# Attention of a hybrid decoder layer: the values become the weights of the probability-times-value product, two heads in the two halves of the array's columns

## The chip, the cores and the metric

The kernel runs on one core of a Trainium2 chip. The metric is the device time of one launch in microseconds (us), the median of several runs. A profiled execution of the same program gives the trace that is read here.

## What is computed

One layer of a decoder, on 1024 prompt tokens and 8 sample tokens, all in float32:

```
z = RMSNorm(x) @ w_in            # q | k | v (12 heads x 64) | u | v_sg | gate_a | gate_b
A: 3 head groups of 4 heads, (window, dilation) = (128,1), (512,4), (2048,16)
   each query reads 129 strided keys; p = softmax(q k / 8); o = p v
   the groups are merged per head slot: y = sum_g softmax_g(logsumexp_g) * o_g
B: gelu(u) * (W_s LayerNorm(gelu(v_sg)) + b)
m = sigmoid(gate_a) * (A @ w_proj_attn) + sigmoid(gate_b) * (B @ w_proj_sg)
x = x + RMSNorm(m @ w_out);  x = x + RMSNorm(SwiGLU(RMSNorm(x)))
```

The change touches only `o = p v` of the prompt tokens and the merge of the groups.

## The kernel before, in words

Every large product runs as three matmuls (high times high, low times high, high times low part, lines 477 to 479 and 894 to 904), which keeps float32 accuracy. These fill TensorE nearly the whole time; what is special to attention is threaded between them.

Attention runs twice, once for each pair of head slots (`pair` 0 and 1); e = 0, 1 is the head of the pair, and lies on partitions 0 to 63 or 64 to 127 of the transposed tensors. The dilated groups 1 and 2 share one order of tokens (residue r of 4, two halves of 128), so that a step T = 0..7 holds 128 queries of group 0 ("near") and 128 queries of groups 1 and 2 together ("far"). For each step T:

- `scores(T)` on TensorE: keys times queries, the two heads in the two halves of the array's rows (lines 620, 624);
- `maxima(T, e)` on VectorE adds the mask, takes the row maxima, and writes the scores into `pr`; `probs(T, e)` on ScalarE is the exponential, in place, with the row sums into `st_at`;
- `turns(T, e)` on TensorE transposes the 3, 4 or 6 blocks of probabilities into PSUM (`psT`); `copy0` and `copy1` on ScalarE bring them to `prT`;
- `pv(T, e)` on TensorE, line 664: weights are the probability block, 128 x 128, and the values, 64 columns, are the moving operand. There are 3 matmuls of a head for T = 0, 4 for T = 2, 4, 6, and 6 for odd T. The trace shows each float32 matmul as two records;
- `outputs(T, e)` on VectorE copies near and far outputs to `ob`, queries on partitions.

Between these, `gates` (24 chunks of three matmuls for each quarter of the gate projection, in groups of three chunks) keeps TensorE busy: nine matmuls stand between `turns(T, 1)` and `pv(T, 0)`. `gate` on ScalarE takes the tanh of a finished gate tile, `gated` on VectorE multiplies it in and, at each third tile, makes the low part of the next weights (`lo_in`, line 1500).

After each pair the near outputs have to be brought into the order of tokens of the far ones. `merge_near` transposes the near `ob` (8 tiles) and the statistics (8 small ones); `merge_place` transposes both back with a stride, which puts them in the far order; VectorE computes the weights of the groups (`merge_weights`, then `merge_sum` after an exponential on ScalarE), multiplies and adds; `merge_out` transposes the sum (8 tiles), and ScalarE writes it to `oaT` in token order. These steps are put between the jobs (j, tg) of the next projection: merge_near after job (0, 1), merge_place after (1, 0), merge_out after (2, 1).

In the second pair VectorE has the sample tokens' key products as well (`k_scores`, lines 1733 and 1735, 24 of them), whose caches GpSimd loads by DMA (line 2086) as products are done, each request behind a wait on `s_kq`; the value caches (line 2098) follow in the same queue. TensorE needs all 24 products after job (3, 2) and all value caches in job (4, 2) (line 805).

What sets the order is the code of each engine, written out by hand; the waits are semaphores.

Of the kernel before, what the change touches and what calls it, by code (L numbers as in the profile page):

```python
# [19 lines left out]
P = 128  # L20
# [96 lines left out]
def build(nc, A, O):  # L117
# [19 lines left out]
    with ctx:  # L137
# [45 lines left out]
        assert _o <= R[4]  # L183
        o0T, _ = at("o0T", [P, SEQ], F32, pr_at)
        srow, _ = at("srow", [4, SEQ], F32, prT_at)
        cv, _o = at("cv", [P, 24, 256], F32, R[3] + 2 * NT * 4)
        assert _o <= R[4]
# [280 lines left out]
        def _(pe):  # L468
# [137 lines left out]
            def attention(pair, U, M):  # L606
# [41 lines left out]

                def pv(T, e):
                    r, hh, N = T // 2, T % 2, 16 * pair + 2 * T + e  # L650
                    hd = slice(HD * e, HD * e + HD)
                    pe.wait_ge(at_c0, N + 1)
                    pe.wait_ge(at_c1, N + 1)
                    if T:
                        pe.wait_ge(at_o, N - 1)
                    if T < 7:

                        pe.wait_ge(at_m, N + 3)
                    near = [vtok[:, t, hd] for t in ((T - 1, T) if T else (T,))]
                    far = [vtok[:, 8 * g + 4 * q + r, hd] for g in (1, 2) for q in range(hh + 1)]  # L660
# [6 lines left out]
                    ins.then_inc(at_pv, 1)  # L667

# [20 lines left out]
                for T in range(8):  # L689
                    gates(12 * T)  # L690
                    if T < 7:
                        scores(T + 1)
                    gates(12 * T + 3)
                    turns(T, 0)
                    gates(12 * T + 6)
                    turns(T, 1)
                    gates(12 * T + 9)
                    pv(T, 0)
                    pv(T, 1)

# [3 lines left out]
            def merge_near(pair):  # L704

                pe.wait_ge(at_o, 16 * pair + 16)
                if pair:
                    pe.wait_ge(s_nc, 5)
                for t in range(8):
                    ins = turn(psT[t // 4][:, P * (t % 4):P * (t % 4) + P], ob[:, 0, t, :])  # L710
                    if t % 4 == 3:
                        ins.then_inc(mg_t, 1)
                for t in range(8):
                    ins = turn(psR[t // 4][0:4, P * (t % 4):P * (t % 4) + P], st_at[:, 0, t, :])
                    if t % 4 == 3:
                        ins.then_inc(mg_t, 1)

            def merge_place(pair):

                pe.wait_ge(mg_a, 2 * pair + 2)  # L720
                pe.wait_ge(mg_d, 2 * pair + 2)
# [4 lines left out]
                for t in range(8):  # L726
                    first = 512 * (t % 2) + t // 2
                    ins = turn(psT[t // 4][:, P * (t % 4):P * (t % 4) + P], o0T[:, first:512 * (t % 2) + 512:4])
                ins.then_inc(mg_p, 1)
# [267 lines left out]
        def _(act):  # L997
# [140 lines left out]
            def attention(pair, U, M):  # L1138
# [33 lines left out]
                for T in range(8):  # L1172
# [3 lines left out]
                    copy1(T, 0)  # L1176
                    if T < 7:
                        probs(T + 1, 0)
# [4 lines left out]
                    if T < 7:  # L1183
                        probs(T + 1, 1)
                    if T % 2:
                        gate((12 * T + 11) // KD)

            def merge_copy(pair):
                act.wait_ge(mg_t, 4 * pair + 1)
                fn(o0T[:, 0:512], psT[0][:, :], ACT.Copy).then_inc(mg_a, 1)  # L1190
                act.wait_ge(mg_t, 4 * pair + 3)
                fn(srow[:, 0:512], psA[0:4, :], ACT.Copy).then_inc(mg_a, 1)
# [4 lines left out]

            def merge_back(pair):
                for hh in range(2):
                    act.wait_ge(mg_o, 2 * pair + hh + 1)  # L1200
                    fn(oaT[:, pair, 512 * hh:512 * hh + 512].rearrange("p (i r) -> p r i", r=4), by4(psR[hh][:, :]), ACT.Copy
                       ).then_inc(mg_done, 1)

            def merge_in(pair, j, tg):
                if (j, tg) == (0, 1):
                    merge_copy(pair)
                elif (j, tg) == (1, 1):
                    merge_exp(pair)
                elif (j, tg) == (2, 1):
                    merge_back(pair)  # L1210

# [278 lines left out]
        def _(dve):  # L1490
# [109 lines left out]
            def attention(pair, U, M):  # L1600
# [27 lines left out]
                def outputs(T, e):  # L1628
                    N = 16 * pair + 2 * T + e
                    dve.wait_ge(at_pv, N + 1)  # L1630
                    v.tensor_copy(ob[:, :, T, HD * e:HD * e + HD], psS[e][0][:, 256:384].rearrange("p (k d) -> p k d", k=2)
                                  ).then_inc(at_o, 1)

                if pair:
                    dve.wait_ge(mg_o, 2)
                maxima(0, 0)
                maxima(0, 1)
                for T in range(8):
                    if T:
                        outputs(T - 1, 0)  # L1640
                        outputs(T - 1, 1)
                    if T < 7:
                        maxima(T + 1, 0)
# [4 lines left out]
                    if T % 2 == 0:  # L1648
                        gated((12 * T + 7) // KD)
                    if T % 2:  # L1650
                        gated((12 * T + 11) // KD)
                outputs(7, 0)
                outputs(7, 1)

            def merge_copy(pair):
                dve.wait_ge(mg_t, 4 * pair + 2)
                v.tensor_copy(o0T[:, 512:SEQ], psT[1][:, :]).then_inc(mg_d, 1)
                dve.wait_ge(mg_t, 4 * pair + 4)
                v.tensor_copy(srow[:, 512:SEQ], psB[0:4, :]).then_inc(mg_d, 1)

            def merge_weights(pair):

                dve.wait_ge(mg_p, 2 * pair + 1)
                st.link(v.tensor_copy(sn[:].rearrange("p t c -> p (t c)"), psC[:, 0:32]))
# [3 lines left out]

            def merge_sum(pair):
                dve.wait_ge(mg_e, pair + 1)  # L1670
# [7 lines left out]
                def spread(kind, t0, n):  # L1678
                    return wt[:, 1 + kind, t0:t0 + n, :].rearrange("p t e -> p (t e)").unsqueeze(2).broadcast_to([P, 2 * n, HD])

                def heads(x):
                    return x.rearrange("p t (e d) -> p (t e) d", e=2)

                st.mark(v.tensor_tensor(heads(ob[:, 1]), heads(ob[:, 1]), spread(1, 0, 8), ALU.mult))
                dve.wait_ge(mg_p, 2 * pair + 2)
                for a in range(2):
                    ins = v.tensor_tensor(heads(ob[:, 0, 4 * a:4 * a + 4]),
                                          psT[a][:, :].rearrange("p (t d) -> p t d", d=HD), spread(0, 4 * a, 4), ALU.mult)
                    if a == 0:
                        st.mark(ins)  # L1690
                st.link(ins)
                v.tensor_tensor(ob[:, 1], ob[:, 1], ob[:, 0], ALU.add).then_inc(mg_w, 1)

            attention(0, U0["gb0"], M0["gb0"])
            for j in range(9):
# [3 lines left out]
                lo_in(U0["qkv1"], 0, 0, j)  # L1699
                if j == 0:  # L1700
                    merge_sum(0)
            kv_copy(1)
# [38 lines left out]
            for j in range(6):  # L1741
                for kk in range(max(8 * j - 8, 0), min(8 * j, 24)):
                    if kk == 2:
                        merge_sum(1)
                    k_scores(kk)
# [432 lines left out]
```

## Time and profile before

| | us |
|---|---|
| median of 3 runs | 1583.19 (1583.07 to 1585.23) |
| the profiled execution | 1582.84 |
| its span, first to last instruction | 1580.9 |
| TensorE busy | 1538.7 (97%) |
| VectorE busy | 543.8 (34%) |
| ScalarE busy | 492.0 (31%) |
| GpSimd busy | 141.4 (9%) |

Busy time of TensorE contains overlap of neighbouring matmuls; a matmul's cost in a row of them is the distance from its start to the next start. The two attention stages are at about 286 to 371 us and 483 to 568 us of the span.

### The profile page before, as it was taken

The page shows a single profiled execution, that of the slowest core. Times are in us where ns is not written, and L with a number is a line of the kernel's source. Part 1 is how long each engine was busy: PE and PEld are TensorE (multiplying, and loading weights), DVE is VectorE, ACT ScalarE, POOL GpSimd, SP SyncE. Part 2 cuts the span into 40 slices and gives each one's busy share as a digit, 9 for nine tenths or more (in the row PEclk, how much of TensorE's full clock was granted, in tenths as well). Part 3 has the DMA queues.
Part 4 walks back from the last instruction along what each step waited for, and adds up shares of the span by engine and source line. Part 5 has one row for each costly group of instructions (what it writes and reads, how often), then busy time and mean ns, then how long its engine had stood idle before and what let it go on. Part 6 is the DMA issues. An engine that isn't in the chain of part 4 may idle for free.

```text
span 1580.9 us, 23134 instructions
## 1 busy us (share of the span) xinstructions
PE 1538.7 (97%) x9881; PEld 1494.2 (95%) x9881; DVE 543.8 (34%) x1016; ACT 492.0 (31%) x951; POOL 141.4 (9%) x172
## 2 busy tenths in 40 slices
PE   5999999999999999999999999999999999999995
PEld 5999999899998999998789999999999999999995
DVE  6104551332214336654652231132122213122236
ACT  5215543443224422336662111211111211121123
POOL 1000000000000025240001101100100110010014
PEclk9999999999999999999999999999999999999998
DMA  6111112100112025134422111111111111111102
GB/s 201 41 53 41 41 41 83 41 28 28 41 41 84 28 83 187 55 107 167 141 80 80 41 54 41 54 41 47 48 52 43 43 51 46 48 42 53 41 27 108
DMA packets 127169, 101.50 MB, mean 64 GB/s; under 512 B 4632, under 2 KB 114208, under 8 KB 127072
## 3 DMA queue, kind: packets, MB, share of 16 engines
q1 hardware_dynamic: 124208, 91.67, 18.7%
q0 software_dynamic: 2720, 7.89, 1.6%
q8 instruction: 75, 1.23, 0.3%
q10 hardware_dynamic: 144, 0.52, 0.1%
q14 instruction: 22, 0.18, 0.0%
HBM read 92.34 MB, written 7.73 MB: 63 GB/s over the span
## 4 chain that ended last, share of the span: by engine, by line
PE 92%; DVE 4%; POOL 1%; issue 1%; DMA 1%; ACT 1%; SPq 0%; ACTq 0%; DVEq 0%; POOLq 0%
PE bank L894 31%; PE bank L477 11%; PE bank L479 10%; PE bank L478 10%; PE bank L902 5%; PE bank L904 5%; PE bank L903 5%; PE psT L473 3%; PE psC L664 1%; PE bank L864 1%; PE bank L863 1%; PE bank L862 1%; PE psA L664 1%; POOL cv L2098 1%; PE psB L624 1%
## 5 line engine op out<-in xcount | busy, mean ns | idle before, releaser
L894 PE MATMUL bank<-f_hi,w_hi 128*128 128x384 f32 (+1 forms) x1056 | 338.6, 321 | 0.2 <-DVE w_lo L1500 0.2
L894 PE MATMUL bank<-f_hi,w_lo 128*128 128x384 f32 (+1 forms) x1056 | 337.8, 320 | 0.0
L894 PE MATMUL bank<-f_lo,w_hi 128*128 128x384 f32 (+1 forms) x1056 | 337.4, 320 | 0.0
L477 PE MATMUL bank<-h_hi,w_hi 128*128 128x344 f32 x1008 | 331.4, 329 | 1.6 <-DVE h_lo L1513 1.4
L1500 DVE TENSOR_TENSOR w_lo<-w_raw,w_hi 128x1024 fp32r<-128x1024 f32 x138 | 169.0, 1225 | 473.7 <-ACT w_hi L1424 226.6
L479 PE MATMUL bank<-h_hi,w_lo 128*128 128x344 f32 x1008 | 322.1, 320 | 0.0
L478 PE MATMUL bank<-h_lo,w_hi 128*128 128x344 f32 x1008 | 321.9, 319 | 0.0
L894 PEld LDWEIGHTS bank<-f_hi,w_hi 128*128 128x128 f32 x1056 | 198.5, 188 | 0.8 <-DVE w_lo L1500 0.5
L894 PEld LDWEIGHTS bank<-f_lo,w_hi 128*128 128x128 f32 x1056 | 198.5, 188 | 0.0
L894 PEld LDWEIGHTS bank<-f_hi,w_lo 128*128 128x128 f32 x1056 | 198.5, 188 | 0.0
L477 PEld LDWEIGHTS bank<-h_hi,w_hi 128*128 128x128 f32 x1008 | 190.0, 189 | 6.3 <-issue 5.0
L478 PEld LDWEIGHTS bank<-h_lo,w_hi 128*128 128x128 f32 x1008 | 189.7, 188 | 0.0
L479 PEld LDWEIGHTS bank<-h_hi,w_lo 128*128 128x128 f32 x1008 | 189.7, 188 | 0.0
L904 PE MATMUL bank<-a_hi,w_lo 128*128 128x384 f32 (+1 forms) x480 | 153.8, 320 | 0.0
L903 PE MATMUL bank<-a_lo,w_hi 128*128 128x384 f32 (+1 forms) x480 | 153.5, 320 | 0.0
L902 PE MATMUL bank<-a_hi,w_hi 128*128 128x384 f32 (+1 forms) x480 | 153.5, 320 | 0.0
L2124 POOL TENSOR_TENSOR a_lo<-sg,a_hi 128x384 fp32r<-128x384 f32 (+1 forms) x66 | 61.6, 934 | 776.7 <-ACT a_hi L1339 776.7
L1424 ACT ACTIVATE w_hi<-w_raw 128x1024 fp32r<-128x1024 f32 x58 | 61.0, 1052 | 202.6 <-PE bank L904 202.6
L1876 DVE TENSOR_TENSOR y<-y,bank 128x384 f32<-128x384 f32 (+1 forms) x120 | 61.1, 510 | 114.6 <-PE bank L904 114.6
L1339 ACT ACTIVATE a_hi<-sg 128x384 fp32r<-128x384 f32 (+1 forms) x66 | 32.5, 492 | 204.9 <-DVE sg L1868 204.9
L902 PEld LDWEIGHTS bank<-a_hi,w_hi 128*128 128x128 f32 x480 | 90.3, 188 | 0.0
L904 PEld LDWEIGHTS bank<-a_hi,w_lo 128*128 128x128 f32 x480 | 90.1, 188 | 0.0
(412 smaller groups left out, 1845.9 us busy)
## 6 DMA issues: line engine op xcount, KB each, us to landing
w_raw<-in_w_in SPq DMA_DIRECT2D x42, 512.0 KB, 3.9
w_raw<-in_w_out SPq DMA_DIRECT2D x24, 512.0 KB, 3.8
w_raw<-in_w_gate SPq DMA_DIRECT2D x23, 512.0 KB, 3.9
w_raw<-in_w_up SPq DMA_DIRECT2D x23, 512.0 KB, 4.0
w_raw<-in_w_down SPq DMA_DIRECT2D x22, 512.0 KB, 3.5
xin<-in_x_prompt SPq DMA_DIRECT2D x8, 512.0 KB, 7.7
xn<-in_x_prompt SPq DMA_DIRECT2D x8, 512.0 KB, 4.8
out_y_prompt<-xn SPq DMA_DIRECT2D x8, 512.0 KB
```

What stands on the lines that cost most here:

```text
L473: return nc.tensor.transpose(out, in_, ident[0:k, 0:k])
L477: mm(out[:, 0:TG], w_hi[par][:, ws], hi[:, k, tgc[tg]], start=first, stop=False)
L478: mm(out[:, 0:TG], w_hi[par][:, ws], lo[:, k, tgc[tg]], start=False, stop=False)
L479: return mm(out[:, 0:TG], w_lo[par][:, ws], hi[:, k, tgc[tg]], start=False, stop=last)
L894: ins = mm(out[:, 0:NG[tg]], w[par][:, ws], x[tg][:, k, :], start=(k == 0 and w is w_hi and x is f_hi), stop=(k == KD - 1 and w is w_lo))
L902: mm(out[:, 0:NG[tg]], hi[:, ws], a_hi[:, k, tgf[tg]], start=(k == 0), stop=False)
L903: mm(out[:, 0:NG[tg]], hi[:, ws], a_lo[:, k, tgf[tg]], start=False, stop=False)
L904: ins = mm(out[:, 0:NG[tg]], lo[:, ws], a_hi[:, k, tgf[tg]], start=False, stop=(k == kc - 1))
L1424: fn(w_hi[j % 2][:], w_raw[j % 2][:], ACT.Copy).then_inc(w_hi_s, 1)
L1500: v.tensor_tensor(w_lo[par][:], w_raw[par][:], w_hi[par][:].bitcast(F32), ALU.subtract).then_inc(w_lo_s, 1)
L1876: v.tensor_tensor(part, part, src[:, 0:NG[tg]], ALU.add).then_inc(free[tg], 1)
L2124: g_.tensor_tensor(a_lo[:, j, tgf[tg]], sg[:, tgf[tg]], a_hi[:, j, tgf[tg]].bitcast(F32), ALU.subtract).then_inc(ff_l, 1)
```

## The change

1. `pv` takes both heads at once. The weights are now the values (128 x 64) and the moving operand is the transposed probability block (128 columns). Head e uses columns 64e to 64e+63 of the array and writes partitions 64e to 64e+63 of its own PSUM bank. The matmuls of the two heads alternate. The output has the head's 64 dimensions on partitions and queries along the free axis, 2 x 128 columns instead of 2 x 64.
2. Since outputs come out transposed, near outputs need no transposes; only the statistics do. Instead the weights of the groups are spread over 64 columns of each head (`wb`, 128 x 2048) and transposed (16 tiles in `merge_out`, now after job (1, 2)). `merge_factors` and `merge_sum` on VectorE multiply and add with the results and write `oaT` themselves.
3. `pv(T)` waits for the copies of both heads and for both heads' maxima of step T+1.
4. ScalarE does the copies of both heads of step T before the exponentials of step T+1. VectorE does `outputs` before the `gated` that makes a low part.

```diff
-                def pv(T, e):
-                    r, hh, N = T // 2, T % 2, 16 * pair + 2 * T + e
-                    hd = slice(HD * e, HD * e + HD)
-                    pe.wait_ge(at_c0, N + 1)
-                    pe.wait_ge(at_c1, N + 1)
+                def pv(T):
+                    r, hh, N = T // 2, T % 2, 16 * pair + 2 * T
+                    pe.wait_ge(at_c0, N + 2)
+                    pe.wait_ge(at_c1, N + 2)
                     if T:
-                        pe.wait_ge(at_o, N - 1)
+                        pe.wait_ge(at_o, N)
                     if T < 7:
-                        pe.wait_ge(at_m, N + 3)
+                        pe.wait_ge(at_m, N + 4)
...
                     for kind, values in enumerate((near, far)):
-                        for a, v in enumerate(values):
-                            ins = mm(psS[e][0][:, 256 + HD * kind:256 + HD * kind + HD], prT[:, e, b, :], v,
-                                     start=(a == 0), stop=(a == len(values) - 1))
+                        for a, t in enumerate(values):
+                            for e in range(2):
+                                hd = slice(HD * e, HD * e + HD)
+                                ins = mm(psS[e][0][hd, 256 + P * kind:256 + P * kind + P], vtok[:, t, hd], prT[:, e, b, :],
+                                         start=(a == 0), stop=(a == len(values) - 1))
...
             def merge_out(pair):
                 pe.wait_ge(mg_w, pair + 1)
-                for hh in range(2):
-                    for r in range(4):
-                        ins = turn(psR[hh][:, P * r:P * r + P], ob[:, 1, 2 * r + hh, :])
-                    ins.then_inc(mg_o, 1)
+                for kind, ps in ((0, psT), (1, psR)):
+                    for t in range(8):
+                        ins = turn(ps[t // 4][:, P * (t % 4):P * (t % 4) + P], wb[:, kind, t, :])
+                        if t % 4 == 3:
+                            ins.then_inc(mg_o, 1)
...
-                elif (j, tg) == (2, 1):
+                elif (j, tg) == (1, 2):
                     merge_out(pair)
...
+                v.tensor_copy(wb[:].rearrange("p k t (e d) -> p (k t e) d", e=2),
+                              wt[:, 1:3].rearrange("p k t e -> p (k t e)").unsqueeze(2).broadcast_to([P, 32, HD])
+                              ).then_inc(mg_w, 1)
...
+                for a in range(2):
+                    dve.wait_ge(mg_o, 4 * pair + a + 1)
+                    part = apart[:, 2 * a:2 * a + 2]
+                    st.mark(v.tensor_tensor(part, part, psT[a][:, :].rearrange("p (r h i) -> p r h i", r=2, h=2), ALU.mult))
...
+                    v.tensor_tensor(oaT[:, pair, half].rearrange("p (i r) -> p i r", r=4),
+                                    near[:, half].rearrange("p (i r) -> p i r", r=4),
+                                    far[:, :, h, :].rearrange("p r i -> p i r"), ALU.add).then_inc(mg_done, 1)
```

On TensorE, at the probability-times-value product of step T = 0 of the first pair (`psA` is the bank of head 0, `psC` of head 1; -, before; +, changed):

```order
 L478 MATMUL bank<-h_lo,w_hi_52 128x344
 L479 MATMUL bank<-h_hi,w_lo_54 128x344
-L664 MATMUL psA<-vtok,prT 128x64 x3
-L664 MATMUL psC<-vtok,prT 128x64 x3
+L665 MATMUL psA<-prT,vtok 64x128
+L665 MATMUL psC<-prT,vtok 64x128
+L665 MATMUL psA<-prT,vtok 64x128
+L665 MATMUL psC<-prT,vtok 64x128
+L665 MATMUL psA<-prT,vtok 64x128
+L665 MATMUL psC<-prT,vtok 64x128
 L477 MATMUL bank<-h_hi,w_hi_52 128x344
```

The number of matmuls stays; the heads now alternate, and the output of each is 64 x 128 instead of 128 x 64.

On ScalarE, step T = 2 before (prT: copies of head 0, then head 1; pr: exponentials of step 3; gt: tanh of a gate tile):

```order
L1154 ACTIVATE prT<-psT 128x256
L1160 ACTIVATE prT<-psT 128x256
L1144 ACTIVATE pr,st_at<-pr,st_at 128x256
L1144 ACTIVATE pr,st_at<-pr,st_at 128x512
L1166 ACTIVATE gt<-bank 128x344
L1154 ACTIVATE prT<-psT 128x256
L1160 ACTIVATE prT<-psT 128x256
L1144 ACTIVATE pr,st_at<-pr,st_at 128x256
L1144 ACTIVATE pr,st_at<-pr,st_at 128x512
```

and the same step of the changed kernel:

```order
L1149 ACTIVATE prT<-psT 128x256
L1155 ACTIVATE prT<-psT 128x256
L1161 ACTIVATE gt<-bank 128x344
L1149 ACTIVATE prT<-psT 128x256
L1155 ACTIVATE prT<-psT 128x256
L1139 ACTIVATE pr,st_at<-pr,st_at 128x256
L1139 ACTIVATE pr,st_at<-pr,st_at 128x512
L1139 ACTIVATE pr,st_at<-pr,st_at 128x256
L1139 ACTIVATE pr,st_at<-pr,st_at 128x512
```

The two exponentials of head 0 have moved behind the copies of head 1.

On VectorE, the merge of the second pair before (wt: the groups' weights; kq: the sample tokens' key products):

```order
L1671 TENSOR_TENSOR wt<-wt,sn 128x16
L1672 TENSOR_TENSOR wt<-wt,st_at 128x16
L1673 TENSOR_TENSOR wt<-wt 128x16
L1674 RECIPROCAL wt<-wt 128x16
L1675 TENSOR_TENSOR wt<-wt 128x16
L1676 TENSOR_TENSOR wt<-wt 128x16
L1684 TENSOR_TENSOR ob<-ob,wt 128x1024
L1687 TENSOR_TENSOR ob<-psT,wt 128x512 x2
L1692 TENSOR_TENSOR ob<-ob 128x1024
L1733 TENSOR_TENSOR kq<-kraw,qb_104 32x256
```

and in the changed kernel the place where the six small instructions end in the spreading copy, before the third key product:

```order
L1655 TENSOR_TENSOR wt<-wt 128x16
L1656 RECIPROCAL wt<-wt 128x16
L1657 TENSOR_TENSOR wt<-wt 128x16
L1658 TENSOR_TENSOR wt<-wt 128x16
L1659 COPY wb<-wt 128x2048
L1727 TENSOR_TENSOR kq<-kraw,qb_104 32x256
```

with the products of the merge six key products and a low part later:

```order
L1484 TENSOR_TENSOR w_lo_54<-w_raw_50,w_hi_52 128x1024
L1672 TENSOR_TENSOR ob<-ob,psT 128x2x256 x2
L1676 TENSOR_TENSOR ob<-ob,psA 128x512
L1676 TENSOR_TENSOR ob<-ob,psB 128x512
L1682 TENSOR_TENSOR oaT<-ob 128x512 x2
L1727 TENSOR_TENSOR kq<-kraw,qb_137 32x256
```

Four instructions ahead of the third product have become a copy there and six instructions ahead of the ninth.

## Rows read from the trace of the kernel before

**Rows 1.** The page, the chain that ended last, by engine.

```profile
PE 92%; DVE 4%; POOL 1%; issue 1%; DMA 1%; ACT 1%; SPq 0%; ACTq 0%; DVEq 0%; POOLq 0%
```

**Rows 2.** Line 664: weight loads, durations min/median/max in ns, starts, forms.

```profile
L664 PEld LDWEIGHTS psC<-vtok,prT x156: 186/192/193, 297.4 to 567.0; 128*128 128x128 f32 x156
```

**Rows 3.** Timeline of TensorE, odd step: start us, us, engine, line, operation.

```profile
502.61 0.32 PE L479 MATMUL bank<-h_hi,w_lo 128*128 128x344 f32 x1
502.77 1.45 PE L664 MATMUL psA<-vtok,prT 128*128 128x64 f32 x12
504.06 1.50 PE L664 MATMUL psC<-vtok,prT 128*128 128x64 f32 x12
505.61 0.32 PE L478 MATMUL bank<-h_lo,w_hi 128*128 128x344 f32 x1
```

**Rows 4.** Timeline of TensorE and VectorE, step T = 2 of the first pair.

```profile
317.17 0.31 PE L479 MATMUL bank<-h_hi,w_lo 128*128 128x344 f32 x1
317.32 1.00 PE L664 MATMUL psA<-vtok,prT 128*128 128x64 f32 x8
317.32 0.17 DVE L1619 TENSOR_SCALAR st_at<-mx 128x2 f32<-128x2 f32 x1
319.26 0.31 PE L478 MATMUL bank<-h_lo,w_hi 128*128 128x344 f32 x1
```

**Rows 5.** Timeline of TensorE, the scores, two heads in row halves.

```profile
495.77 0.32 PE L479 MATMUL bank<-h_hi,w_lo 128*128 128x344 f32 x1
496.02 0.48 PE L620 MATMUL psA<-qk 64*128 64x256 f32 x1
496.02 0.48 PE L620 MATMUL psC<-qk 64*128 64x256 f32 x1
...
496.77 0.27 PE L624 MATMUL psB<-qk 64*128 64x128 f32 x1
...
496.89 0.27 PE L624 MATMUL psB<-qk 64*128 64x128 f32 x1
...
497.35 0.32 PE L478 MATMUL bank<-h_lo,w_hi 128*128 128x344 f32 x1
```

**Rows 6.** Timeline, the sample tokens' product in four column strips.

```profile
629.16 1.07 PE L805 MATMUL psB<-cv,spT 128*32 128x256 f32 x16 [0.40 <-DMA cv<-in_cache_win]
630.02 1.07 PE L805 MATMUL psC<-cv,spT 128*32 128x256 f32 x16
```

**Rows 7.** Line 805: weight loads, durations min/median/max in ns, starts.

```profile
L805 PEld LDWEIGHTS psB<-cv,spT x16: 106/109/110, 629.1 to 629.6; 128*32 128x32 f32 x16
```

**Rows 8.** Timeline of TensorE, transposes of the merge, first pair.

```profile
388.64 1.23 PE L473 MATMUL psT<-ident,o0T 128*128 128x128 f32 x8
...
404.80 0.60 PE L473 MATMUL psA<-ident,ob 128*128 128x128 f32 x4
405.24 0.60 PE L473 MATMUL psB<-ident,ob 128*128 128x128 f32 x4
```

**Rows 9.** Timelines, first merge: VectorE, and TensorE's start of job (2, 0).

```profile
395.37 1.22 DVE L1684 TENSOR_TENSOR ob<-ob,wt 128x1024 f32<-128x1024 f32 x1
...
397.25 0.32 PE L477 MATMUL bank<-h_hi,w_hi 128*128 128x344 f32 x1
```

**Rows 10.** Groups of VectorE by form: busy us, mean ns.

```profile
L1542 DVE TENSOR_SCALAR iom<-iot 128x256 int32<-128x256 int32 x1 | 0.3, 282 | 0.0
```

**Rows 11.** Timelines, second merge and key products: VectorE, and TensorE after job (3, 2).

```profile
592.82 0.17 DVE L1671 TENSOR_TENSOR wt<-wt,sn 128x16 f32<-128x16 f32 x1 [2.14 <-ACT wt L1196]
...
597.52 0.40 DVE L1733 TENSOR_TENSOR kq<-kraw,qb 32x256 f32<-32x256 f32 x1
...
603.32 0.41 DVE L1733 TENSOR_TENSOR kq<-kraw,qb 32x256 f32<-32x256 f32 x1
...
611.21 0.42 DVE L1733 TENSOR_TENSOR kq<-kraw,qb 128x256 f32<-128x256 f32 x1 [2.38 <-DMA qb<-q_rows]
...
619.89 0.57 PE L473 MATMUL psC<-ident,sst 128*32 128x128 f32 x6
```

More of the change, by code:

```diff
@@ L718, in merge_place @@
             def merge_place(pair):
-                pe.wait_ge(mg_a, 2 * pair + 2)
-                pe.wait_ge(mg_d, 2 * pair + 2)
+                pe.wait_ge(mg_a, pair + 1)
+                pe.wait_ge(mg_d, pair + 1)
                 for t in range(8):
@@ L1630, in outputs @@
                     dve.wait_ge(at_pv, N + 1)
[L1631 to L1635, printed above, removed]
+                    hd = slice(HD * e, HD * e + HD)
+                    v.tensor_copy(ob[hd, :, T, :], psS[e][0][hd, 256:512].rearrange("p (k i) -> p k i", k=2)).then_inc(at_o, 1)
                 maxima(0, 0)
@@ L1641, in attention @@
                         outputs(T - 1, 1)
+                    if T and T % 2 == 0:
+                        gated((12 * T - 1) // KD)
                     if T < 7:
@@ L1649, in attention @@
                         gated((12 * T + 7) // KD)
[L1650 to L1651 removed]
                 outputs(7, 0)
                 outputs(7, 1)
+                gated(95 // KD)
             def merge_copy(pair):
[L1656 to L1658 removed]
+                dve.wait_ge(mg_t, 2 * pair + 2)
                 v.tensor_copy(srow[:, 512:SEQ], psB[0:4, :]).then_inc(mg_d, 1)
             def merge_weights(pair):
[L1663 removed]
+                dve.wait_ge(mg_p, pair + 1)
                 st.link(v.tensor_copy(sn[:].rearrange("p t c -> p (t c)"), psC[:, 0:32]))
@@ L1667, in merge_weights, with merge_factors @@
                 v.tensor_tensor(wt[:, 2], wt[:, 0], st_at[:, 1, :, 0:2], ALU.subtract).then_inc(mg_r, 1)
-            def merge_sum(pair):
+            def merge_factors(pair):
                 dve.wait_ge(mg_e, pair + 1)
@@ L1676, in merge_sum @@
                 st.link(v.tensor_tensor(wt[:, 2], wt[:, 2], wt[:, 3], ALU.mult))
[L1678 to L1685, printed above, removed]
-                for a in range(2):
-                    ins = v.tensor_tensor(heads(ob[:, 0, 4 * a:4 * a + 4]),
-                                          psT[a][:, :].rearrange("p (t d) -> p t d", d=HD), spread(0, 4 * a, 4), ALU.mult)
+                v.tensor_copy(wb[:].rearrange("p k t (e d) -> p (k t e) d", e=2),
+                              wt[:, 1:3].rearrange("p k t e -> p (k t e)").unsqueeze(2).broadcast_to([P, 32, HD])
+                              ).then_inc(mg_w, 1)
+            def merge_sum(pair):
+                near = ob[:, 0].rearrange("p t q -> p (t q)")
+                far = ob[:, 1].rearrange("p (r h) i -> p r h i", h=2)
+                apart = near.rearrange("p (h i r) -> p r h i", h=2, r=4)
+                for a in range(2):
+                    dve.wait_ge(mg_o, 4 * pair + a + 1)
+                    part = apart[:, 2 * a:2 * a + 2]
+                    st.mark(v.tensor_tensor(part, part, psT[a][:, :].rearrange("p (r h i) -> p r h i", r=2, h=2), ALU.mult))
+                for a in range(2):
+                    dve.wait_ge(mg_o, 4 * pair + a + 3)
+                    part = ob[:, 1, 4 * a:4 * a + 4, :].rearrange("p t i -> p (t i)")
+                    ins = v.tensor_tensor(part, part, psR[a][:, :], ALU.mult)
                     if a == 0:
@@ L1691, in merge_sum @@
                 st.link(ins)
-                v.tensor_tensor(ob[:, 1], ob[:, 1], ob[:, 0], ALU.add).then_inc(mg_w, 1)
+                for h in range(2):
+                    half = slice(512 * h, 512 * h + 512)
+                    v.tensor_tensor(oaT[:, pair, half].rearrange("p (i r) -> p i r", r=4),
+                                    near[:, half].rearrange("p (i r) -> p i r", r=4),
+                                    far[:, :, h, :].rearrange("p r i -> p i r"), ALU.add).then_inc(mg_done, 1)
             attention(0, U0["gb0"], M0["gb0"])
```

38 lines of the change are left out of this document (12 added, 26 removed).

## The prediction

> **What bounds the kernel now.** I read the chain that ended last first: 92% of it is TensorE [rows 1]. So an edit counts by what it takes from or adds to TensorE's stream, or by a wait it puts there. The second view was TensorE's timeline in the attention stages, read by distances between starts. Two matmuls of the gate product start 0.16 us apart; what stands between them costs the distance less 0.32 us (two such steps, L479 to L478). For an odd step, pv runs from 502.61 to 505.61: 3.00 - 0.32 = 2.68 us for 24 records, 0.112 each [rows 3]. An even step costs 319.26 - 317.17 - 0.32 = 1.77 us for 16 records [rows 4]. The waits on others are in the timelines of VectorE and the second merge [rows 4, 11].
>
> **Why pv costs that.** Each record moves 64 columns but loads a weight block of 128 columns; the load's record lasts 192 ns [rows 2] and one is finished each 0.107 us (12 records from 502.77 to 504.06, rows 3). The price is that of the loads. The other way round there are as many records, each with 64 columns to load and 128 to move. Alone that would win nothing. All hangs on whether the two heads, in different columns of the array, run at once.
>
> **Part 1, two heads at once.** Two places of this kernel bear on it. The scores put the heads in the two halves of the rows: both first matmuls start at 496.02, and one round of 128 columns for both heads goes from 496.77 to 496.89 [rows 5]. The sample product puts four sequences in four column strips with four different moving operands: 16 records of 256 columns from 629.16 to 630.02, four rounds of 0.215 us, so four strips run in the time of one [rows 6]. That is 0.107 us for a round of 128 columns, in the column layout that the change uses.
>
> The loads could still bind. In the sample product a load lasts 0.109 us [rows 7], and the 16 start between 629.1 and 629.6, so the later ones lie beside matmuls. Two loads of 64 columns are together what one load of 128 is now, 0.107 us [rows 3]: at worst, one after the other but beside the matmuls, they fill the round exactly. I take 0.107 us for a round.
>
> Changing the array's layout costs something. The scores of a step, from 495.77 to 497.35, are 1.58 us; less 0.32, and less the rounds (four of 128 columns and two of 256, 8 x 0.107 = 0.86), leaves 0.40 us [rows 5]. I charge this to each pv; its bounds are 0 and 0.40, since a plain excursion shows part of it already.
>
> The new pv: odd step 12 rounds, 1.28 + 0.40 = 1.68 us; T = 2, 4, 6 8 rounds, 0.86 + 0.40 = 1.26; T = 0 6 rounds, 0.64 + 0.40 = 1.04.
>
> **Part 2, the new wait in pv.** pv now wants both heads' maxima of step T+1. For even T these are 512 columns wide, and the write of `st_at` for head 1 starts at 317.32 and lasts 0.17, while pv starts at 317.32 [rows 4]. So pv waits some 0.2 us in each even step (0 to 0.3). Behind it stand the gate matmuls, so it counts in full. In odd steps the maxima are 256 wide and end before pv. Both heads' copies have come ahead of the exponentials on ScalarE, so they are earlier than now. The exponentials, some 1.3 us later, are wanted by the next step's transposes, behind pv, scores and six gate matmuls; I cost that at nothing. The longer output copies (256 columns for 128) and the moved `gated` have nine gate matmuls, 1.4 us, ahead of the next waiter; nothing either.
>
> Sum for pv, 16 steps: odd 8 x (2.68 - 1.68) = 8.0; even but 0: 6 x (1.77 - 1.46) = 1.9; T = 0: before 12 x 0.112 = 1.34, now 1.24, 2 x 0.1 = 0.2. Gain 10.1 us.
>
> **Part 3, the merge.** Removed per pair: 8 near transposes, at 0.11 us each (four from 404.80 to 405.24), and 8 in `merge_place`, 1.23 less the last one's tail of 0.16, 1.07 us [rows 8]. `merge_out` has 16 for 8, +0.88. Net 0.88 + 1.07 - 0.88 = 1.1 us a pair, 2.2 in all.
>
> `merge_out` comes two jobs earlier. The six small instructions end at 395.37; then the spreading copy, 2048 elements wide. TensorE is at the place at 397.25 [rows 9]. No row has such a copy. Bounds: 1024 elements with two sources take 1.22 us [rows 9], so at one a cycle it is some 2.3 us; a one-source instruction of 256 elements takes 0.282 [rows 10], which against 0.40 for two sources of the same width [rows 11] is twice the rate, some 1.2 us. I take 1.2, from the nearest in kind: ready at 396.6, no wait. At 2.3 it is ready at 397.7 and TensorE waits 0.45 us in each pair.
>
> The Trainium skill ("VectorE: DVE Perf Modes", The perf-mode tier table) gives 2x to an fp32 copy within SBUF, 1227 ns at 2048 elements, and 1x to fp32 tensor_tensor; rows 9 and 10 fit both, but none has a source that is repeated 64 times. By the page the wait is nothing, by the upper bound the sum is 0.9 less.
>
> **Part 4, the sample tokens' chain.** In the second pair the third key product waits for the merge, 597.52 - 592.82 = 4.70 us; the ninth runs at 603.32 [rows 11]. Now the merge starts 1.1 us sooner (`merge_place` is shorter), and 1.1 for the small instructions and 1.2 for the copy give a third product at 594.0; six products of 0.78 and a low part of 1.14 end at 599.8; six instructions of 512 wide, about 3.8 us (half of 1.22 each), put the ninth at 603.6, 0.3 later than now. From the ninth hang query load and key loads on GpSimd's queue, then the value loads. TensorE is meanwhile 0.3 us earlier (1.07 less, 0.88 less, 1.76 more). It waits for the value caches already [rows 6], and passes the point after job (3, 2) at 619.89, just behind the last key product [rows 11]. So 0.6 us is lost. Bounds: with a copy of 2.3 us the ninth is 1.2 late, 1.5 lost; if the query's transfer, which the 15th product awaits at 611.21 [rows 11], lands sooner because the loads ahead of it are more spread, nothing is lost and 0.5 gained.
>
> **Sum.** 10.1 + 2.2 - 0.6 = 11.7 us. The profiled execution took 1582.84 (span 1580.9, 1.9 around it), so 1571.1; the median of the runs shown is 0.35 above it: 1571.5.
>
> **Rivals.** A, the forecast: 1571.5. Chance 0.63.
>
> B, weight loads do not lie beside matmuls in the column layout. For it: the pair shares its rows, and rows 5 show the overlap for split rows only. Against it: the loads of rows 7 start inside the matmuls of rows 6. Price: a load of 64 columns lies between 109 ns (32 columns, rows 7) and 192 (128, rows 2), some 135 ns, for 156 rounds 21 us: 1592.5, slower. It decides above 0.075 us a round.
> The Trainium skill ("TensorE: Matmul & The Clock Gate", Part 3, The mechanism) states B's rule: LDWEIGHTS overlaps with matmuls in flight only when the row group differs. The trace does not agree with it in rows 6 and 7, though these are four strips of 32. By the page B is right, by the rows A. 0.05.
>
> C, the two halves run one after the other (wide strips with 128 x 64 weights are not in the trace; four narrow ones are): 156 x 0.107 = 16.7 us more, 1588.2, slower. 0.05.
>
> D, both merge waits and the sample chain at their upper bounds: 0.9 + 0.9 more, 1573.3. It is near to certain to remain faster. 0.13.
>
> E, the layout change mostly hidden behind the load that stands ahead: 16 x 0.25 = 4 us more gained, 1567.5. The scores speak against it, and 0.40 there was measured. 0.08.
>
> F, loads beside matmuls but partly exposed, 0.05 us a round: 156 x 0.05 = 8 us, 1579.5. 0.06.
>
> **Range and chances.** 1567 to 1579 holds A, D and E; B, C, most of F and odd ends are left out, some 0.18. A run tells 0.2%, about 3.2 us, from no change. Faster: A, D, E and half of F, 0.87; same: 0.03; slower: B and C, 0.10.
>
> **What would show it.** Right: in TensorE's timeline an odd pv some 1.7 us from L479 to the second gate matmul less 0.32, records of psA and psC starting in pairs each 0.107; 0.2 us of wait on `st_at` in even steps; `merge_out` starting without a wait on `wb`, whose copy is near 1.2 us; a wait for `cv` of about 1 us before the sample product. Wrong: pairs 0.16 to 0.24 us apart (F, B), or psC starting when psA ends (C); transposes that wait for `pr`.

## The result

| | us |
|---|---|
| before, median of 4 runs | 1583.13 (1582.41 to 1585.23) |
| changed, median of 4 runs | 1571.49 (1570.99 to 1572.4) |
| ratio | 0.9926 [0.9914, 0.9938] |
| forecast | 1571.5 (1567 to 1579) |
| profiled execution of the changed kernel | 1571.74, span 1569.9 |

The change makes the kernel faster by 11.6 us, 0.74%. The forecast came out to the tenth, which is partly luck: three of its terms were off, and the rest was made up by stretches that the change does not touch.

The table below follows landmarks of TensorE's timeline through both profiled executions, from the start of one piece to the start of the next.

| stretch of TensorE | before | after | gained |
|---|---|---|---|
| start of the span to the first scores | 286.61 | 287.82 | -1.21 |
| attention, first pair | 91.59 | 86.39 | 5.20 |
| `merge_near` to `merge_place` | 9.39 | 8.52 | 0.87 |
| `merge_place` to the second gate matmul behind it | 2.28 | 1.31 | 0.97 |
| from there to the next projection's transposes (`merge_out`) | 88.37 | 89.23 | -0.86 |
| these transposes to the first scores of the second pair | 5.53 | 5.54 | -0.01 |
| attention, second pair | 92.98 | 87.40 | 5.58 |
| `merge_near` to `merge_place`, second pair | 9.38 | 8.53 | 0.85 |
| `merge_place` to the sample tokens' product | 43.03 | 42.46 | 0.57 |
| sample tokens' product to the end | 951.74 | 952.70 | -0.96 |

The stretches that the change touches gained 13.2 us. The first and the last, whose code is the same, took 2.2 us longer in this execution. The span lost 11.0.

How long these two outer stretches take differs between executions: together 1238.3 us in the one profiled execution of the kernel before, 1238.5 to 1241.1 in the ten of the changed kernel and its variants. The part between them, from the first scores to the sample tokens' product, repeats closely: 329.39 and 329.34 us in the two profiled executions of the changed kernel, against 342.56 before. So 13.2 us is what the touched part gained, and 11.6 is what the medians show; whether the outer stretches are really slower after the change, one execution of before cannot tell.

### The profile page after: what moved, and what is told of

Its sections match the earlier page's. It is cut to its first block, busy times and chain, and to the rows that moved or that the text cites. A ratio compares the mean times of both kernels' runs of the same rounds, so it can differ in the third digit from the quotient of the medians.

```text
span 1569.9 us, 23072 instructions
## 1 busy us (share of the span) xinstructions
PE 1527.2 (97%) x9865; PEld 1475.8 (94%) x9865; DVE 553.4 (35%) x1020; ACT 487.7 (31%) x945; POOL 141.7 (9%) x172
## 3 DMA queue, kind: packets, MB, share of 16 engines
q8 instruction: 75, 1.23, 0.3%
## 4 chain that ended last, share of the span: by engine, by line
PE 93%; DVE 4%; DMA 1%; issue 1%; ACT 1%; SPq 0%; POOL 0%; DVEq 0%; ACTq 0%
PE bank L889 31%; PE bank L477 12%; PE bank L479 11%; PE bank L478 11%; PE bank L897 5%; PE bank L899 5%; PE bank L898 5%; PE psT L473 2%; PE psA L665 1%; PE bank L859 1%; PE bank L858 1%; PE bank L857 1%; DVE pr L1596 1%; PE psB L624 1%; DMA xin<-in_x_prompt 1%
## 5 line engine op out<-in xcount | busy, mean ns | idle before, releaser
L479 PE MATMUL bank<-h_hi,w_lo 128*128 128x344 f32 x1008 | 322.6, 320 | 0.0
L479 PEld LDWEIGHTS bank<-h_hi,w_lo 128*128 128x128 f32 x1008 | 190.1, 189 | 0.0
```

The source lines that it names most:

```text
L479: return mm(out[:, 0:TG], w_lo[par][:, ws], hi[:, k, tgc[tg]], start=False, stop=last)
```

## The profile after

TensorE still sets the end. On the page: the chain that ended last by engine, and the busy times (compare [rows 1]).

```profile
PE 93%; DVE 4%; DMA 1%; issue 1%; ACT 1%; SPq 0%; POOL 0%; DVEq 0%; ACTq 0%
...
PE 1527.2 (97%) x9865; PEld 1475.8 (94%) x9865; DVE 553.4 (35%) x1020; ACT 487.7 (31%) x945; POOL 141.7 (9%) x172
```

TensorE's busy time fell by 11.5 us, the span by 11.0: TensorE has that much less work, and does not merely wait less.

The instructions of the new pv by line (duration ns min/median/max, first and last start, forms), against [rows 2]:

```profile
L665 PEld LDWEIGHTS psC<-prT,vtok x156: 132/137/137, 298.3 to 556.3; 128*64 128x64 f32 x156
L665 PE MATMUL psC<-prT,vtok x156: 272/273/323, 298.3 to 556.4; 128*64 128x128 f32 x156
```

and two of these loads in the timeline of an odd step:

```profile
497.78 0.14 PEld L665 LDWEIGHTS psA<-prT,vtok 128*64 128x64 f32 x1
497.78 0.14 PEld L665 LDWEIGHTS psC<-prT,vtok 128*64 128x64 f32 x1
```

There are as many records of a head as before, 156. A load lasts 137 ns where it lasted 192, and the loads of the two halves start together.

TensorE's timeline, an odd step, against [rows 3], and step T = 2 of the first pair, against [rows 4] (start us, us, engine, line, operation, and in brackets the idle time before it and its releaser):

```profile
317.21 0.31 PE L479 MATMUL bank<-h_hi,w_lo 128*128 128x344 f32 x1
317.68 0.29 PE L665 MATMUL psA<-prT,vtok 128*64 128x128 f32 x1 [0.15 <-DVE st_at L1603]
...
318.97 0.32 PE L478 MATMUL bank<-h_lo,w_hi 128*128 128x344 f32 x1
...
497.37 0.32 PE L479 MATMUL bank<-h_hi,w_lo 128*128 128x344 f32 x1
497.62 0.32 PE L665 MATMUL psA<-prT,vtok 128*64 128x128 f32 x1
497.62 0.32 PE L665 MATMUL psC<-prT,vtok 128*64 128x128 f32 x1
497.78 0.27 PE L665 MATMUL psA<-prT,vtok 128*64 128x128 f32 x1
497.78 0.27 PE L665 MATMUL psC<-prT,vtok 128*64 128x128 f32 x1
497.88 0.27 PE L665 MATMUL psA<-prT,vtok 128*64 128x128 f32 x1
...
498.87 0.27 PE L665 MATMUL psC<-prT,vtok 128*64 128x128 f32 x1
499.08 0.43 PE L477 MATMUL bank<-h_hi,w_hi 128*128 128x344 f32 x1
499.34 0.32 PE L478 MATMUL bank<-h_lo,w_hi 128*128 128x344 f32 x1
```

psA and psC start together, and rounds lie 0.107 to 0.109 us apart. The odd pv takes 499.34 - 497.37 - 0.32 = 1.65 us where it took 2.68, the even one 318.97 - 317.21 - 0.32 = 1.44 where it took 1.77. At both ends of the twelve rounds one sees the change of layout: the first matmul starts 0.25 us after the last of the gates instead of 0.16, the second round 0.16 after the first, the next gate matmul 0.21 after the last round, and the one behind it 0.26 after that. Together that is 0.35 us more than evenly spaced matmuls would take, and 0.37 with the rounds between, which are a little over 0.107.

TensorE's waits in the attention and merge stages, 270 to 660 us (total us, times, longest us), first rows:

```profile
PE psA L665 <- DVE st_at L1603: 1.2, 8, 0.2
PE psA L620 <- DVE st_at L1603: 1.1, 1, 1.1
```

The first is the change's new wait: 0.15 us in each step with wide maxima. The second was 1.4 us in two waits before; one of them, 0.28 us at 486.61, is down to 0.14 and too short to show in this view. No wait on `wb`, `ob` or `cv` appears.

VectorE's timeline around the merge: the spreading copy of the first pair, and in the second pair the products of the merge and the key products behind them, against [rows 9, 11].

```profile
389.55 1.23 DVE L1659 COPY wb<-wt 128x2048 f32<-128x2048 f32 x1
...
588.51 2.08 DVE L1672 TENSOR_TENSOR ob<-ob,psT 128x512 f32<-128x512 f32 x2
590.46 0.72 DVE L1676 TENSOR_TENSOR ob<-ob,psA 128x512 f32<-128x512 f32 x1
591.06 0.72 DVE L1676 TENSOR_TENSOR ob<-ob,psB 128x512 f32<-128x512 f32 x1
591.81 2.10 DVE L1682 TENSOR_TENSOR oaT<-ob 128x512 f32<-128x512 f32 x2
593.82 0.41 DVE L1727 TENSOR_TENSOR kq<-kraw,qb 32x256 f32<-32x256 f32 x1
...
599.27 0.40 DVE L1727 TENSOR_TENSOR kq<-kraw,qb 128x256 f32<-128x256 f32 x1
```

The copy takes 1.23 us, as taken. The six instructions of the merge take 5.31 us (588.51 to 593.82), not 3.8. Four of them, those of L1672 and L1682, are not plain: L1672 reads and writes `ob` with a stride of four elements, L1682 reads one operand in steps of 256 elements, four at a time. They take 0.97 to 1.01 us from start to start for 512 elements, where the first plain one takes 0.60. But nothing waits for the query's transfer, which held up a key product by 2.38 us before [rows 11].

TensorE at the sample tokens' product, against [rows 6]:

```profile
616.96 0.31 PE L479 MATMUL bank<-h_hi,w_lo 128*128 128x344 f32 x1
617.20 1.07 PE L800 MATMUL psB<-cv,spT 128*32 128x256 f32 x16
```

The wait for `cv` has gone: 0.24 us lie between the two starts, where 629.16 - 628.45 = 0.71 lay before.

## The experiments

All are edits of the changed kernel. It ran again in the second group (labelled `changed_again`): 1571.3 us, ratio 0.992 [0.9906, 0.9934].

| run | median us | ratio to the kernel before | against changed | touched part of the trace, against changed |
|---|---|---|---|---|
| `e1_heads_in_turn` | 1581.64 | 0.9987 [0.9978, 0.9997] | +10.2 | +10.6 |
| `e2_exponentials_between` | 1574.33 | 0.9948 [0.9931, 0.9964] | +2.9 | +2.7 |
| `e3_low_part_before_outputs` | 1579.93 | 0.998 [0.997, 0.999] | +8.5 | +9.6 |
| `e4_pv_beside_scores` | 1567.11 | 0.9896 [0.9879, 0.9912] | -4.3 | -4.1 |
| `e4_again` | 1566.59 | 0.989 [0.9875, 0.9905] | -4.7 | -4.1 |
| `e5_merge_out_later` | 1576.06 | 0.9956 [0.994, 0.9971] | +4.7 | +3.2 |
| `e6_pv_in_two_visits` | 1571.76 | 0.9925 [0.9911, 0.9938] | +0.4 | +0.6 |
| `e7_heads_by_twos` | 1571.4 | 0.9928 [0.9911, 0.9945] | 0.0 | +0.5 |

The fourth column is the difference of medians against 1571.4, the middle of the changed kernel's two medians. The last is the part of the profiled execution from the first scores to the sample tokens' product, less 329.4; it does not hold the scatter of the outer stretches. e1 to e4 ran on one chip (kernel before 1583.85), e4_again to e6 and the changed kernel on another (1583.33), e7 on a third (1582.64).

### Heads one after the other

```diff
...
-                    for kind, values in enumerate((near, far)):
-                        for a, t in enumerate(values):
-                            for e in range(2):
...
+                    for e in range(2):
...
+                        for kind, values in enumerate((near, far)):
+                            for a, t in enumerate(values):
...
```

> The changed kernel, with the matmuls of head 0 all ahead of those of head 1 in each pv; numbers, tiles and waits are the same. Theory A-strict (matmuls start in program order, so two heads share a round only where they alternate): each head takes its own rounds, 156 x 0.107 = 16.7 us more, about 1588. Rival (each column half works through its own matmuls from a look-ahead of several instructions): the heads still run side by side and the time stays near 1571.5; in TensorE's timeline psC starts with psA. In between: only the look-ahead's depth is shared, and the loss is a part of 16.7 us.

It lost 10.2 us, between the two theories. TensorE's timeline of an odd step of this kernel:

```profile
501.34 0.32 PE L479 MATMUL bank<-h_hi,w_lo 128*128 128x344 f32 x1
501.59 1.20 PE L665 MATMUL psA<-prT,vtok 128*64 128x128 f32 x9
502.52 0.32 PE L665 MATMUL psC<-prT,vtok 128*64 128x128 f32 x1
502.62 0.27 PE L665 MATMUL psA<-prT,vtok 128*64 128x128 f32 x1
502.68 0.27 PE L665 MATMUL psC<-prT,vtok 128*64 128x128 f32 x1
...
502.90 1.15 PE L665 MATMUL psC<-prT,vtok 128*64 128x128 f32 x9
503.97 0.42 PE L477 MATMUL bank<-h_hi,w_hi 128*128 128x344 f32 x1
```

The first record of head 1 starts beside the ninth of head 0, the last of the nine merged in the second line. Three more of head 0 follow between those of head 1, then head 1 runs alone: some 20 rounds where twelve would do. In the even steps the first record of head 1 stands beside the fifth of eight, in T = 0 beside the third of six, so in each kind of step the last four of head 0 overlap. With four in each step, 156 - 16 x 4 = 92 rounds of 0.107 us are added, 9.8 us; the medians show 10.2 and the trace's pv blocks 10.6 (34.9 for 24.3), some 0.05 us more in each step. The two halves do run at once, but only when the instruction stream brings both near each other. Where head 1 is alone it has one load in a round and still needs 0.109 us for it, as two heads do: the second half's load adds nothing.

### Heads by twos

```diff
...
-                        for a, t in enumerate(values):
+                        for a0 in range(0, len(values), 2):
                             for e in range(2):
...
+                                for a in range(a0, min(a0 + 2, len(values))):
...
```

> The changed kernel with the heads alternating after every two matmuls (four records) instead of every one. In e1 the first record of head 1 ran beside the ninth of twelve of head 0, so four records ahead are looked at. Theory (look-ahead of four records): head 1's first record still starts with head 0's first, nothing is lost: within 0.7 us of the changed kernel, 0.9926 of the kernel before. Rival (in e1 the last four overlapped only because nothing of head 0 was left to load): each swap costs a round or two, 3 to 8 us more.

1571.4 us, as the changed kernel. This kernel's timeline of TensorE, where the heads follow each other in blocks of four records:

```profile
497.45 0.27 PE L666 MATMUL psC<-prT,vtok 128*64 128x128 f32 x1
497.51 0.27 PE L666 MATMUL psA<-prT,vtok 128*64 128x128 f32 x1
497.56 0.27 PE L666 MATMUL psC<-prT,vtok 128*64 128x128 f32 x1
497.62 0.27 PE L666 MATMUL psA<-prT,vtok 128*64 128x128 f32 x1
```

Each head still has a record each 0.11 us, half a round apart. An odd pv costs 1.70 us in the trace for 1.66, all sixteen 24.8 for 24.3: two matmuls (four records) in a row cost next to nothing, 0.5 us that the median does not show. That agrees with the count from e1.

### The exponentials back between the copies

```diff
+                    if T < 7:
+                        probs(T + 1, 0)
...
-                        probs(T + 1, 0)
```

> The changed kernel with ScalarE's old order: the exponential of head 0 of step T+1 stands between the copies of head 0 and head 1 of step T. Theory: in even steps the copies of head 1 end at about 0.8 us after pv could start (the 512-wide exponentials take 1.2 us there), so TensorE waits for them some 0.4 us beyond the wait on the maxima, in 6 to 8 of 16 steps: 2.5 to 3.5 us slower than the changed kernel, 1574 to 1575. Rival: the copies' place is free, since the maxima are the later of the two: within 0.5 us of 1571.5.

It lost 2.9 us. TensorE's waits, 270 to 660 us, first row:

```profile
PE psA L665 <- ACT prT L1155: 4.1, 8, 0.5
```

In eight steps pv waits 0.51 us for the copy of head 1, in place of 0.15 for `st_at`: 4.1 - 1.2 = 2.9 us. The median's 2.9 rests on four runs that scatter from 1572.5 to 1576.34. The profiled one is the lowest, 0.8 us above the changed kernel's, because its outer stretches were 2.0 us shorter; its touched part is 2.7 us longer. So the part of the change on ScalarE is worth nearly 3 us.

### The low part before the outputs

```diff
-                    if T and T % 2 == 0:
-                        gated((12 * T - 1) // KD)
...
+                    if T % 2:
+                        gated((12 * T + 11) // KD)
...
-                gated(95 // KD)
```

> The changed kernel with VectorE's old order: in odd steps the gated product with the low part of the next weights stands before the output copies. Theory: the low part ends 4.0 us after pv starts, the copies 0.9 later, and the scores of two steps later could start 3.1 us after pv starts, so TensorE waits some 1.9 us in steps 1, 3 and 5 of each pair: 11 to 12 us slower than the changed kernel, about 1583, the whole gain gone. Rival: the gate chunks cover it as they did before, loss under 1 us.

It lost 8.5 us by the medians and 9.6 in the touched part of the trace, some 2 to 3 less than expected: a wait is 1.52 us, not 1.9. TensorE's waits, 270 to 660 us:

```profile
PE psA L620 <- DVE ob L1616: 9.2, 6, 1.5
PE psA L665 <- DVE st_at L1603: 1.2, 8, 0.2
```

and the second of the six places in the timelines of VectorE and of TensorE:

```profile
330.28 1.23 DVE L1484 TENSOR_TENSOR w_lo<-w_raw,w_hi 128x1024 fp32r<-128x1024 f32 x1 [0.43 <-ACT w_hi L1000]
331.42 0.41 DVE L1616 COPY ob<-psA 64x256 f32<-64x256 f32 x1
331.86 0.43 DVE L1616 COPY ob<-psC 64x256 f32<-64x256 f32 x1
...
332.44 0.45 PE L620 MATMUL psA<-qk 64*128 64x256 f32 x1 [1.52 <-DVE ob L1616]
```

With the old order on VectorE the low part stands ahead of both copies, and the next scores need the banks. The kernel before has this order too and no such wait in it: there the copies, 0.28 us each, end at 331.32 and the scores start at 331.54, just in time. In e3 the last gate matmul starts at 330.60, 0.7 us sooner since pv is shorter, and the copies, 0.42 us each, end at 332.29, 1.0 later. So the old order no longer fits the shorter pv; without the reordering most of the gain is lost.

### pv directly behind the scores

```diff
-                        pe.wait_ge(at_o, N - 2)
+                        if T >= 2:
+                            pe.wait_ge(at_o, N - 4)
...
+                    if T:
+                        pv(T - 1)
...
-                    pv(T)
+                pv(7)
```

> The changed kernel with pv(T-1) right behind scores(T+1) (both use halves of the array) instead of behind the last gate chunks of step T-1; the scores wait for the outputs of one step earlier. Theory: one of four crossings between layouts goes in each of 14 steps, 0.2 us each, and the wait on the maxima (8 x 0.15 to 0.2) goes too: 3.5 to 4.5 us faster than the changed kernel, 1567 to 1568. Rival 1: row halves to column halves is a crossing as dear as two: only the waits go, 1570. Rival 2: the outputs, a step part later on VectorE, hold up the scores or the maxima: slower than the changed kernel.

The fastest kernel of this study: 4.3 us under the changed kernel on the first chip, 4.7 on the second, where both ran. Its timeline where the scores (heads in row halves) give way to pv (column halves):

```profile
497.34 0.38 PE L625 MATMUL psB<-qk 64*128 64x256 f32 x1
...
497.65 0.32 PE L666 MATMUL psA<-prT,vtok 128*64 128x128 f32 x1
497.66 0.32 PE L666 MATMUL psC<-prT,vtok 128*64 128x128 f32 x1
497.81 0.27 PE L666 MATMUL psA<-prT,vtok 128*64 128x128 f32 x1
```

From 497.34 to 497.81 are 0.47 us; a round of 256 columns (0.215) and one of 128 (0.107) account for 0.32. The crossing costs 0.15 us, and saves leaving for the gates and coming back. The wait on `st_at` ahead of pv is gone as well, 1.2 us in all. The trace's touched part is 4.1 us shorter, so 2.9 are left for the crossings. They are saved in twelve steps, not fourteen: behind the last scores of a pair pv(6) still stands between gate matmuls. That is 0.24 us a step where the expectation had 0.2.

> e4 again beside the changed kernel on one chip: 4 to 5 us faster than it, as found from their ratios to the kernel before (0.9896 and 0.9926). The profile has no wait on st_at before pv.

> The changed kernel itself, as the base for e4, e5 and e6 on the same chip: 11 to 12 us faster than before (0.9926). If it comes out at 13 us, the first profile's count in the changed stages (13 us gained there, 2 lost elsewhere) is the better measure.

The two medians lie 4.7 us apart, the touched parts of the traces 4.1, as in the first pair of runs. The changed kernel is 12.0 us under the kernel before here, which is nearer to the first medians' 11.6 than to 13; its touched part is again 329.3 us long.

### pv in two visits

e4 with the near and the far products separated by three gate matmuls, in 14 places (only the added separation is shown):

```diff
+                        pv(T - 1, (0,))
+                    gates(12 * T + 3, 1)
+                    if T:
+                        pv(T - 1, (1,))
...
```

> The kernel of e4 with the near and far matmuls of pv apart by one gate chunk, so that TensorE leaves the column halves and comes back once more in each of 14 steps; matmuls and chunks are the same in number. Theory: leaving and coming back cost 0.40 us together, as the scores showed: 5.6 us slower than e4, some 1572.5. Rival: most of the 0.40 is the drain behind a single long block and is paid less for a short one: 0.2 a visit, 2.8 us. If a crossing cost nothing, e4's gain would be the waits alone and this one would equal e4.

5.2 us above `e4_again`, 0.37 for each further visit; in the traces' touched parts 4.7 and 0.33. TensorE's timeline of one:

```profile
500.72 0.27 PE L668 MATMUL psC<-prT,vtok 128*64 128x128 f32 x1
500.92 0.43 PE L477 MATMUL bank<-h_hi,w_hi 128*128 128x344 f32 x1
501.19 0.32 PE L478 MATMUL bank<-h_lo,w_hi 128*128 128x344 f32 x1
501.34 0.32 PE L479 MATMUL bank<-h_hi,w_lo 128*128 128x344 f32 x1
501.59 0.32 PE L668 MATMUL psA<-prT,vtok 128*64 128x128 f32 x1
...
501.75 0.27 PE L668 MATMUL psA<-prT,vtok 128*64 128x128 f32 x1
```

From the last round of the first visit to the second round of the next are 1.03 us; three gate matmuls take 0.47 and two rounds 0.22, so leaving and coming back costs 0.34. The change of layout is real and is paid each time. Rival E, by which most of it is hidden, falls.

### merge_out two jobs later

```diff
-                elif (j, tg) == (1, 2):
+                elif (j, tg) == (2, 1):
```

> The changed kernel with merge_out back behind job (2, 1). Nothing is added or removed. Theory (the sample tokens' chain is close behind TensorE): in the second pair merge_sum on VectorE stands before the ninth key product and now waits for the transposes until about 592.5, so this product and all behind it come 3 us later than at 593.8; TensorE waits after job (3, 2) or before the sample product: 2.5 to 4 us slower than the changed kernel. Rival: the chain has room again, since the query's transfer is no longer awaited: same time within 0.5 us.

The median is 4.7 us above the changed kernel, with a wide scatter (1574.68 to 1578.23). TensorE's waits, 560 to 660 us:

```profile
PE psC L473 <- DVE sst L1744: 2.4, 1, 2.4
...
PE psB L800 <- DMA cv<-in_cache_win: 0.6, 1, 0.6
```

Neither wait is in the changed kernel. They sum to 3.0 us, which is what this kernel's profiled execution (1574.68) stands above the changed kernel's (1571.74). The rest of the 4.7 us shows in other executions only and stays open. The touched part is 3.2 us longer. The early place of `merge_out` is needed for the sample tokens, not for TensorE: the merge's products then lie ahead of the ninth key product instead of further down the chain.

## Why the prediction was right

**Two heads at once (part 1): right.** Rival C (halves in turn) and B (loads exposed) would show as psC starting only when psA ends, or rounds well over 0.107 us. They start within 0.01 to 0.04 us of each other. In F the 0.05 us a round was to be seen in 156 rounds; 0.002 at most is. The estimate of 135 ns for a 64-column load was met by 137, and two such loads in each 0.109 us do not stretch the round. Their records start together and lie beside the matmuls, and one load in a round takes as long (e1), so the loads of the halves overlap each other and the matmuls. The Trainium skill ("TensorE: Matmul & The Clock Gate", Part 3, The mechanism) lets LDWEIGHTS overlap matmuls in flight only where the row group differs; here both halves use all rows, and by that rule the kernel would have been slower than before, as rival B has it. The rows above decide against it for two column halves.

That the old pv was bound by its weight loads, as the prediction reads it, was not tested by a run. What speaks for it are the transposes of `merge_place` in the changed kernel, which move four columns against weights of 128 columns:

```profile
382.73 1.12 PE L473 MATMUL psC<-ident,srow 4*128 4x4 f32 x8
```

The next gate matmul starts at 383.78, so each of the eight takes 0.13 us, no less than a record of the old pv with its 64 columns (0.112).

**The price of the layout: right.** 0.40 us was taken, and 0.37 is seen in the odd step. Rival E, which had most of it hidden, falls by that. In the odd steps it gives 1.65 us for the 1.68 forecast, in even steps 1.44 for 1.46 with a wait of 0.15 for the 0.2. Two visits instead of one cost 0.33 to 0.37 us each in e6.

**The sum for pv: 10.1 forecast, 10.8 measured.** Read from L479 to the second gate matmul, less 0.32, the sixteen pv cost 35.0 us before and 24.3 after. The odd steps gave 8 x (2.68 - 1.65) = 8.2. The even ones gave 2.3, more than 6 x (1.77 - 1.44) = 2.0, since one of the six took 1.98 us before instead of the 1.77 of the step that the prediction read. The two of T = 0 gave 0.3 instead of 0.2.

**The orders on ScalarE and VectorE: costed at nothing, rightly, and necessary.** No wait on `prT` or `ob` appears in the profile after. e2 and e3 show what the old orders would have cost: 2.9 and 8.5 us. The cover that the prediction named, nine gate matmuls, is gone if a low part of 1.2 us stands ahead of the copies.

**The merge: 2.2 forecast, 1.9 measured** (0.87 + 0.97 - 0.86 in the first pair, 0.85 + 0.97 - 0.87 in the second). The near transposes saved 0.86 rather than 0.88, the place 0.97 for 1.07. The spreading copy took 1.23 us for the 1.2 taken, and TensorE did not wait. The Trainium skill ("VectorE: DVE Perf Modes", The perf-mode tier table) gives 1227 ns for an fp32 copy of this width, and the trace agrees, also with a source that repeats.

**The sample tokens' chain: the sign was wrong.** 0.6 us lost was forecast, about 0.5 was gained, and the wait of about 1 us for `cv` that was named as a sign is not there. Counted from the start of `merge_place`, the third key product came when forecast (582.70 + 11.4 = 594.1 for 594.0). The six instructions of the merge were taken as half of a plain one each, 3.8 us; they took 5.31, and the ninth product came 1.9 us later than before (593.82 against 603.32 - 11.4) where 0.3 was forecast. TensorE was put 0.3 us earlier; the terms given, 1.07 + 0.88 - 1.76, make 0.19, and 0.10 was measured. Against this stood the query's transfer, which the prediction gave as a bound only. It was awaited 2.38 us before the product at 611.21, which is the 16th and not the 15th, and is no longer: that transfer landed 6.6 us after its issue before and 3.9 after. The third product starts earlier, and the key and query loads are issued over 583 to 601 us instead of 598 to 612. The value loads were issued from 600.76, 16.4 us ahead of the sample tokens' product, where it had been 16.7 us (612.44 to 629.16), and still the wait of 0.40 us for them went: the last of them landed 3.3 us after its issue where it took 4.2. Why they landed sooner, and whether the spread loads are the reason for the query's, no run tested; that stays open. How near this chain is to the path was: with `merge_out` two jobs later, e5, TensorE waits 3.0 us on it. The forecast had the better sign only as a bound, so that it came out this way is luck.

**What cancelled.** pv was 0.7 and the sample chain 1.1 us better than forecast, the merge 0.3 worse, and 2.2 us more went in the outer stretches, which are the same in both kernels: 11.7 + 1.5 - 2.2 = 11.0, the span's gain. The four runs of the two kernels spread over 2.8 and 1.4 us, so a tenth's agreement tells nothing.

## What to carry to other kernels

Where a stream of small matmuls is bound by weight loads of 128 columns, make the small operand the weights and put two independent problems in the halves of the columns; alternate them at least every two matmuls. Enter and leave a split layout as rarely as possible: put such products next to each other instead of spreading them between full-width ones. Joining two heads' work makes the later one's copies and reads a wait for both, so look at what stands ahead of them on each helper engine, and move long instructions with distant waiters behind.

## What the runs showed of the hardware

- Matmuls in two column halves overlap only when they are near each other in the stream: four records of each half in a row cost 0.04 us in an odd pv of 1.66 (e7), and of six, eight or twelve in a row only the last four overlap (e1).
- A visit to column halves costs 0.33 to 0.37 us beyond its matmuls (the changed kernel, e6), a crossing from row halves to column halves 0.15 (e4).
- A float32 multiply of 512 elements (one operand in PSUM) with a stride of four elements in an operand and the output takes 0.97 to 0.99 us from start to start, an add in SBUF with one operand read in steps of 256 elements 1.01, a plain multiply with PSUM 0.60; a float32 copy in SBUF whose source repeats each element 64 times runs at the rate of a plain one, 2048 elements in 1.23 us.
